# Three of the modulation vectors weighed on VectorE, the latents' squares added before the matmul, and a token-wise final norm

## What is computed

```python
for l in range(2):
    sh1, sc1, g1, sh2, sc2, g2 = split(silu(c) @ w_mod[l] + b_mod[l], 6)   # latents
    mod_c = silu(c_ctx) @ w_mod[l] + b_mod[l]                              # context, all six only in layer 0
    xn = rmsnorm(h, norm1_g[l]) * (1 + sc1) + sh1                          # xnc likewise
    proj = xn @ w_in[l]               # pooling, Hyena, q and kv latents, gates
    q = rmsnorm(c_q, q_norm_g[l]) @ w_uq[l]; kv = rmsnorm(c_kv, kv_norm_g[l]) @ w_ukv[l]
    h = h + g1 * token_mix(...)       # three branches, gated, then w_out
    h = h + g2 * (relu((rmsnorm(h, norm2_g[l]) * (1 + sc2) + sh2) @ w_ff1[l]) ** 2 @ w_ff2[l])
return rmsnorm(h, final_g)
```

## Time and profile before

| | |
|---|---|
| median of 3 runs | 1388.97 us (1387.62 to 1389.35) |
| the profiled execution: its time, its span | 1388.05 us, 1386.2 us |
| PE, PE weight load, DVE, ACT, POOL busy (us) | 1352.0, 1109.7, 779.5, 549.4, 195.1 |
| chain that ended last, by engine | PE 92%, DVE 3%, ACT 2%, DMA 1%, issue 1% |
| mean granted clock of PE | 0.994 |

### The profile page before, as it was taken

One profiled execution on the slowest core, in us unless ns is written; L12 is line 12 of the kernel. 1 busy time (PEld: TensorE's weight loads), 2 busy tenths in 40 slices (PEclk: granted clock), 3 DMA queues, 4 the chain that ended last, 5 costly groups with the idle time before them and its releaser, 6 DMA issues.

```text
span 1386.2 us, 19645 instructions
## 1 busy us (share of the span) xinstructions
PE 1352.0 (98%) x8084; PEld 1109.7 (80%) x8084; DVE 779.5 (56%) x1127; ACT 549.4 (40%) x849; POOL 195.1 (14%) x179
## 2 busy tenths in 40 slices
PE   7999999999999999999999999999999999999997
PEld 3567766778778886877778888888779999899996
DVE  5555575234448666543223443477866788765663
ACT  5652472332233323432112432143555445553552
POOL 1251000703100142000000002300005404100012
PEclk9999999999999999999999999999999999999998
DMA  9333303444531372345443235324325647455551
GB/s 374 119 131 114 107 1 141 155 167 160 205 107 61 122 263 102 107 152 183 152 143 109 98 117 214 124 81 140 107 79 190 223 138 278 143 190 185 184 195 62
DMA packets 55289, 205.28 MB, mean 148 GB/s; under 512 B 6261, under 2 KB 6645, under 8 KB 53664
## 3 DMA queue, kind: packets, MB, share of 16 engines
q1 hardware_dynamic: 52992, 194.22, 40.4%
q0 software_dynamic: 2208, 9.81, 2.0%
HBM read 200.86 MB, written 3.15 MB: 147 GB/s over the span
## 4 chain that ended last, share of the span: by engine, by line
PE 92%; DVE 3%; ACT 2%; DMA 1%; issue 1%; POOL 0%; SPq 0%; DVEq 0%; ACTq 0%
PE ps L1556 27%; PE ps L1558 26%; PE ps L1557 26%; PE ps L1868 2%; PE ps L1585 2%; PE ps L1879 1%; DMA pairs<-in_pairs 1%; PE ps L1894 1%; PE ps L1966 1%; PE ps L1978 1%; DVE wl L1040 1%; PE ps L1810 1%; PE ps L1706 1%; PE ps L1610 1%; DVE rstd L1078 0%
## 5 line engine op out<-in xcount | busy, mean ns | idle before, releaser
L1040 DVE TENSOR_TENSOR wl<-raw,wh 128x1024 fp32r<-128x1024 f32 (+2 forms) x272 | 353.5, 1302 | 220.4 <-ACT wh L723 217.1
L1556 PE MATMUL ps<-xh,wh 128*128 128x512 f32 (+2 forms) x1392 | 474.3, 341 | 2.2 <-DVE xl L1107 1.4
L1557 PE MATMUL ps<-xl,wh 128*128 128x512 f32 (+2 forms) x1392 | 466.5, 335 | 0.0
L1558 PE MATMUL ps<-xh,wl 128*128 128x512 f32 (+2 forms) x1392 | 466.3, 335 | 0.0
L723 ACT ACTIVATE wh<-raw 128x1024 fp32r<-128x1024 f32 (+2 forms) x272 | 283.7, 1043 | 321.5 <-PE ps L1558 320.4
L1556 PEld LDWEIGHTS ps<-xh,wh 128*128 128x128 f32 (+1 forms) x1392 | 261.0, 188 | 44.7 <-issue 14.7
L1558 PEld LDWEIGHTS ps<-xh,wl 128*128 128x128 f32 (+1 forms) x1392 | 261.4, 188 | 29.2
L1557 PEld LDWEIGHTS ps<-xl,wh 128*128 128x128 f32 (+1 forms) x1392 | 262.0, 188 | 28.0 <-issue 1.2
L1556 PE MATMUL ps<-hid_h,wh 128*128 128x512 f32 (+1 forms) x512 | 172.5, 337 | 0.0
L1557 PE MATMUL ps<-hid_l,wh 128*128 128x512 f32 (+1 forms) x512 | 171.7, 335 | 0.0
L1558 PE MATMUL ps<-hid_h,wl 128*128 128x512 f32 (+1 forms) x512 | 171.6, 335 | 0.0
(11 more groups left out here) (252 smaller groups left out, 1441.7 us busy)
## 6 DMA issues: line engine op xcount, KB each, us to landing
raw<-in_units SPq DMA_DIRECT2D x262, 512.0 KB, 3.3
...
```

Of the source, the lines that this page charges most:

```text
L1040: dve.tensor_tensor(wl[:, g % SLOTS, 0:n], raw[:, g % SLOTS, 0:n], wh[:, g % SLOTS, 0:n].bitcast(F), ALU.subtract)\
L1556: pe.matmul(dst, w_h, m_h, start=first, stop=False)
L1557: pe.matmul(dst, w_h, m_l, start=False, stop=False)
L1558: return pe.matmul(dst, w_l, m_h, start=False, stop=last)
```

## The change

Three separate edits.

1. Of the ten modulation vectors, numbers 7, 8 and 9 (`SUMMED`: layer 1's first scale, first gate, second shift) are weighed on DVE. For each of a vector's eight units DVE multiplies the 128x1024 unit by the silu column and adds it into an accumulator (`weigh`); vector 7 is needed for both streams and takes two such operations a unit, 8 and 9 one: 32 in all. Then PE adds up the partitions with a 128x32 matrix that holds one column of ones (`mod_sum`, 8 matmuls for vector 7, 4 for the others). The patterns of layer 0 change: no modulation in `ff1a`, one weighing behind each of the 16 units of `ff2a` and the first 8 of `ff2b`, three sums (`s`), and a tail of 8 units (vector 10 on PE) where there were 13. A ring slot comes free when its unit is weighed, so SP waits on that.
2. DVE adds up the latents' squares (two additions for q, one for kv), and PE sums one block where it summed three and two, and 4 columns where it made 8.
3. The last norm is made token by token: PE turns the gained blocks (16 transposes), sums squares into one column a token block, ACT takes two roots of 128x1, DVE one reciprocal of 128x2, and DVE and ACT each scale half of the output from PSUM and store it, in four pieces from SP and ACT.

```diff
-            return pattern if first else pattern.replace("m", "").replace("t", "")
+            return pattern if first else pattern.replace("m", "").replace("t", "").replace("s", "")
...
-            ("ff1a", with_mods("MMMMMMMMmmMMMmmMMMmmMMmm")), ("ff2a", with_mods("MMmmMMMmmMMMmmMMMmmMMmmMMMm")),
-            ("ff1b", 16 * "M"), ("ff2b", 16 * "M" + with_mods(13 * "t")),
+            ("ff1a", with_mods("MMMMMMMMMMMMMMMM")), ("ff2a", with_mods("MmMmMmMmMmMmMmMmMmMmMmMmsMmMmMmMm")),
+            ("ff1b", 16 * "M"), ("ff2b", with_mods("MmMmMmMmsMmMmMmMmMMMMsMMMM" + 8 * "t")),
...
+            elif kind == "s":
+                p.after[j].append(("sum", mod // KB - 1))
+                p.after[j].append(("copy", mod // KB - 1))
+                order.append(("sum", mod // KB - 1))
+                turn, lead = mod // KB - 1, 0
+            elif mod // KB in SUMMED:
+                p.after[j].append(("weigh", mod))
+                order.append(("unit", mod))
+                mod += 1
...
-GAP_SLOTS = {i: (layer, name, slot) for layer, name, count in ((0, "w_out", 14), (0, "ff2b", 11), (1, "w_out", 6))
+GAP_SLOTS = {i: (layer, name, slot) for layer, name, count in ((0, "w_out", 14), (0, "ff2b", 8), (1, "w_out", 6))
...
-GAP_COUNTS = {(0, "w_out"): 14, (0, "ff2b"): 25, (1, "w_out"): 31}
+GAP_COUNTS = {(0, "w_out"): 14, (0, "ff2b"): 22, (1, "w_out"): 28}
...
+        weighted_of = {7: gained[:, :, :].rearrange("p a b -> p (a b)").rearrange("p (s c) -> p s c", c=D),
+                       8: final[:, 0:1, :], 9: final[:, 1:2, :]}
...
-                        sp.wait_ge(mod_done, RING[RING.index(i) - MOD_SLOTS] - MOD_FIRST + 1)
+                        before = RING[RING.index(i) - MOD_SLOTS]
+                        if before // KB in SUMMED:
+                            sp.wait_ge(weighed, weighed_before(before) + streams_of(before // KB))
+                        else:
+                            sp.wait_ge(mod_done, DONE["unit", before])
...
-            pieces = (slice(0, 4), slice(4, 6), slice(6, 8))
-            for piece in pieces:
-                for m in range(piece.start, piece.stop):
-                    await_normed(sp, 2 * DEPTH, m)
-                sp.dma_start(out[:, piece, :], gained[:, piece, :]).then_inc(out_stored, 16)
-            sp.wait_ge(out_stored, 16 * len(pieces))
+            for tb in range(SEQ // 128):
+                sp.wait_ge(final_dve, tb + 1)
+                sp.dma_start(out[tb, :, 0:512], final[:, tb, 0:512]).then_inc(out_stored, 16)
+            sp.wait_ge(out_stored, 16 * (SEQ // 64))
...
+                act.wait_ge(mod_done, DONE["sum", v] if v in SUMMED else DONE["unit", KB * v + KB - 1])
...
+                if v == 2 * DEPTH:
+                    for tb in range(SEQ // 128):
+                        act.activation(rstd[:, tb:tb + 1], ps[:, tb, 0:1], ACT.Sqrt, bias=eps[:, 0:1], scale=1.0 / D).then_inc(std_ready, 1)
+                    return
...
+            act.wait_ge(rstd_ready, parts_before(2 * DEPTH) + 1)
+            act.wait_ge(gain_turned, 1)
+            for tb in range(SEQ // 128):
+                act.activation(final[:, tb, 512:D], ps[:, FINAL_BANK[tb][1], :], ACT.Copy, scale=rstd[:, tb:tb + 1]).then_inc(final_act, 1)
+            for tb in range(SEQ // 128):
+                act.wait_ge(final_act, tb + 1)
+                act.dma_start(out[tb, :, 512:D], final[:, tb, 512:D]).then_inc(out_stored, 16)
...
+            def weigh(i):
+
+                v, k = divmod(i, KB)
+                before = weighed_before(i)
+                if k == 0:
+                    dve.wait_ge(mod_done, DONE["unit", KB * SUMMED[0] - 1])
+                weight, loaded, value = mod_slot(i)
+                dve.wait_ge(loaded, value)
+                for st in range(streams_of(v)):
+                    acc, by = weighted_of[v][:, st, :], silu_wide[:, k, st:st + 1]
+                    if k == 0:
+                        dve.tensor_scalar(acc, weight, by, None, ALU.mult).then_inc(weighed, 1)
+                    else:
+                        dve.wait_ge(weighed, before - streams_of(v) + st + 1)
+                        dve.scalar_tensor_tensor(acc, weight, by, acc, ALU.mult, ALU.add).then_inc(weighed, 1)
 
             def add_mod(v):
...
-                        dve.wait_ge(mod_done, GAP_XL_LAST - MOD_FIRST + 1)
+                        dve.wait_ge(mod_done, DONE["unit", GAP_XL_LAST])
...
-                v = 2 * DEPTH
-                norm_rstd(v)
-                for m in range(KB):
-                    if m not in BY_POOL:
-                        dve.wait_ge(gain_ready, m + 1)
-                        dve.tensor_tensor(gained[:, m, :], gained[:, m, :], rstd[:, 0:SEQ], ALU.mult).then_inc(normed_dve, 1)
+                count = parts_before(2 * DEPTH)
+                dve.wait_ge(std_ready, count + 2)
+                dve.reciprocal(rstd[:, 0:2], rstd[:, 0:2]).then_inc(rstd_ready, 1)
+                dve.wait_ge(rstd_ready, count + 1)
+                dve.wait_ge(gain_turned, 1)
+                for tb in range(SEQ // 128):
+                    dve.tensor_scalar(final[:, tb, 0:512], ps[:, FINAL_BANK[tb][0], :], rstd[:, tb:tb + 1], None, ALU.mult)\
+                       .then_inc(final_dve, 1)
...
+                def add_queries():
+                    chained(dve.tensor_tensor(lat_sq[:, 0, 0:n], lat_sq[:, 0, 0:n], lat_sq[:, 1, 0:n], ALU.add))
+                    dve.tensor_tensor(lat_sq[:, 0, 0:n], lat_sq[:, 0, 0:n], lat_sq[:, 2, 0:n], ALU.add).then_inc(lat_added, 1)
+
+                def add_keys():
+                    dve.wait_ge(lat_sq_ready[layer], QB + KVB)
+                    dve.tensor_tensor(lat_sq[:, QB, :], lat_sq[:, QB, :], lat_sq[:, QB + 1, :], ALU.add).then_inc(lat_added, 1)
...
                             split(WAVE + i + 1)
+                    add_queries()
+                    add_keys()
...
                             i += 1
+                    add_queries()
+                    add_keys()
...
+            def mod_sum(v):
+
+                vectors_ready(pe, v - 1)
+                if v == SUMMED[0]:
+                    pe.wait_ge(picks_ready, 2)
+                pe.wait_ge(weighed, weighed_before(KB * v) + KB * streams_of(v))
+                for st in range(streams_of(v)):
+                    for j in range(4):
+                        mm = pe.matmul(ps[32 * j:32 * j + 32, mod_bank(v), 0:MOD_COLS], picks[:, 1 - st:33 - st],
+                                       weighted_of[v][:, st, j * MOD_COLS:(j + 1) * MOD_COLS], start=st == 0, stop=st == streams_of(v) - 1)
+                mm.then_inc(mod_done, 1)
...
+            def turn_gained(m):
+                pe.wait_ge(gain_ready, m + 1)
+                for tb in range(SEQ // 128):
+                    mm = pe.transpose(ps[:, FINAL_BANK[tb][m // 4], m % 4 * 128:m % 4 * 128 + 128], gained[:, m, tb * 128:(tb + 1) * 128], ident)
+                return mm
+
+            def final_sums(v):
+
+                def by_token(squares, first, last):
+                    for tb in range(SEQ // 128):
+                        mm = pe.matmul(ps[:, tb, 0:1], squares[:, tb * 128:(tb + 1) * 128], ones[:, 0:1], start=first, stop=last)
+                    return mm
+
+                for m in range(KB - 2):
+                    turn_gained(m)
+                pe.wait_ge(act_bank_free, drained(DEPTH - 1, "ff1b"))
+                pe.wait_ge(squares_added, added_before(v + 1))
+                by_token(sq_sum, True, False)
+                pe.wait_ge(h_squared, squared_before(v + 1))
+                by_token(sq[:, 0, :], False, False)
+                turn_gained(KB - 2)
+                pe.wait_ge(last_squared, v)
+                by_token(sq[:, 1, :], False, True).then_inc(sumsq_ready, 1)
+                turn_gained(KB - 1).then_inc(gain_turned, 1)
...
-                for first, count, bank, nt in ((0, QB, 4, n), (QB, KVB, 5, T)):
-                    pe.wait_ge(lat_sq_ready[layer], first + count)
-                    for k in range(count):
-                        mm = pe.matmul(ps[:, bank, 0:nt], ones, lat_sq[:, first + k, 0:nt], start=k == 0, stop=k == count - 1)
-                    mm.then_inc(lat_sumsq[layer], 1)
+                for i, bank, nt in ((0, 4, n), (QB, 5, T)):
+                    pe.wait_ge(lat_added, 2 * layer + (2 if i else 1))
+                    pe.matmul(ps[:, bank, 0:nt], ones, lat_sq[:, i, 0:nt], start=True, stop=True).then_inc(lat_sumsq[layer], 1)
                 for tb in range(T // 128):
-                    for k in range(KVB):
-                        mm = pe.matmul(ps[:, 7, tb:tb + 1], lat_sq[:, QB + k, tb * 128:(tb + 1) * 128], ones[:, 0:1],
-                                       start=k == 0, stop=k == KVB - 1)
+                    mm = pe.matmul(ps[:, 7, tb:tb + 1], lat_sq[:, QB, tb * 128:(tb + 1) * 128], ones[:, 0:1], start=True, stop=True)
                 mm.then_inc(lat_sumsq[layer], 1)
...
-                rms(2 * layer + 2)
                 if layer == 0:
```

(3 more changed lines are left out.)

49 lines of the change are left out of this document (30 added, 19 removed).

## The result

The changed kernel takes 1376.64 us (median of 4 runs, 1376.35 to 1377.87), the kernel before 1389.16 beside it. The ratio is 0.9915, with a 95% interval of 0.9901 to 0.9929: 11.8 us faster by the ratio. 1369.2 was forecast, so 7.4 us are missing, and the time lies outside the range.

The account below looks back on a forecast made before the run. PE, busy 98% of the span, was taken as the bound. 9.4 + 1.0 + 6.0 + 1.6 + 2.0 = 20.0 us off the profiled 1388.05 gave 1368.0, or 1369.2 for the median; range 1366.5 to 1375.

Parts of the forecast that it names:

- a unit of 24 is 5.44 us: Layer 0's `ff2a`: PE starts a weight matmul every 0.227 us, so 24 take 5.44 us, with no wait.
- not free, or the units cost nothing: Rival, 0.03: the weighing isn't free or the units cost nothing where they stood; PE waits elsewhere, so no change.
- The inline units and the tail: Modulation units leaving `ff1a` and `ff2a` gain 9.4 us; eight tail units instead of 13 between the layers gain 1.0.
- The weighing: DVE's 32 operations of 128x1024 take 1.3 us each; DVE keeps up, cost on the path 0.
- Latents, layer 0: At layer 0's latents' sums three wide and four narrow matmuls leave PE: 3.4 us gained, nothing waits.
- 0.75 each at most: Layer 0: DVE's two q additions, 0.75 us each at most, fall into its 1.47 us wait for ACT.
- Layer 1: At layer 1's latents' sums PE sheds matmuls worth 2.6 us; a late DVE could eat up to 1 us.
- the rival with VectorE as the bound: Rival, 0.12: DVE's additions and reciprocals become layer 1's bound; the tail's 1.0 and 1.0 of the sums go: 1371.2.
- The clock: Behind layer 1's sums PE's clock no longer falls, because the change halves the thin stretch ahead: 1.6 us gained.
- The rival's fall in a new place: Rival, 0.25: the clock falls anyway or newly, with PE waiting in layer 1's first wave: 1370.8 or 1372.4.
- The end: The last norm, token by token: first store at 1379.15 instead of 1381.20, gain 2.0 us.
- The low bound: The last norm's gain is only 0.5 us, because ACT's first DMA of the kernel is slow.

Follow-up runs that it names:

- e1: The changed kernel with the new buffer `picks` allocated behind all others, so every other buffer stands where it stood before the change: 0.9872 of the kernel before.
- e2: The kernel before with only an unused buffer of 144 bytes a partition behind `wl`, which moves the buffers behind it as the change does: 1.0069.
- e8: e1 with 28 of the weighings cut to 8 of 1024 columns: 0.9861 of the kernel before.
- e3: The kernel before with only the addition of the latents' squares on DVE, no buffer moved: 0.9956.
- e13: e1 with layer 0's keys' addition placed behind `ckl` on VectorE: 0.9855 of the kernel before.
- e9: e1 with the four one-column matmuls at the latents' sums issued twice each: 0.9875 of the kernel before.
- e15: e1 with the wide float32 sums issued five times and the one-column matmuls twice, as before the change: 0.9902 of the kernel before.
- e5: The kernel before with an unused buffer of 64 bytes a partition behind `wl`: 1.0014.
- e7: The kernel before with only the token-wise last norm: 0.9982.
- e6: e1 without the token-wise last norm: 0.9885 of the kernel before.
- e12: e1 measured once more, the same program: 0.9864 of the kernel before.

## Why the prediction was wrong

**The step that failed** is in the part on the bound: "a unit of 24 is 5.44 us", with 0.227 us a step, was carried over into the changed kernel as a constant, and what the diff does to the other buffers' addresses was put at nothing. The step depends on where the operands lie, and the diff moves them (e1, e2). By the table, after against e1 loses 2.5 us up to 540 us (`cq`, `ck`, `fh`), 2.8 in `ff2a` and 2.8 in `ff2b`. In layer 1 the 767 steps on `hid` cost 0.0022 more each, 1.7 us, which shorter steps on `xh` more than covered this time. By the ratios it is 0.0043 to 0.0051, 6 to 7 us of the 7.4. None of my rivals had it: "not free, or the units cost nothing" looked for a wait, and there is none.

**The inline units and the tail:** 9.4 + 1.0 forecast. In e1 the saving goes from 4.3 at 540 us to 14.1 ahead of layer 1's sums: 9.8. It is made of 11.4 up to `ff2b`, 2.5 lost on its two sums and turns, 1.4 won in the tail and 0.6 lost between layer 1's first weight matmul and its sums. The sum of vector 7 stands 1.33 us apart from its neighbours (700.68 to 702.01) where a pair stood 1.32. **The weighing:** 1.3 taken, 1.28 measured, cost on the path 0, shown by e8. One of 28 took over the 2 us that the prediction named as a sign of being wrong (2.31, beside GpSimd); e8, which shortens it too, shows that it cost nothing. **The tail:** PE waits for `xl` as described, but starts 0.26 us behind its end at 911.35, where 0.1 was forecast.

**Latents, layer 0:** 3.4 forecast, 2.5 measured (e3 and the table). The step that fell is "0.75 each at most" for the additions "into the 1.47 us": beside GpSimd's rows they took 1.67 to 1.79, against 0.68 for the same shape in layer 1 with GpSimd idle, and I had not seen that the sums' own bank waits for `ckl`. The earlier trace rows had shown the price, 1.99 for 1.32. The Trainium skill ("SBUF — State Buffer", "SBUF: two separate sides") says that a VectorE operation with two SBUF inputs and a GpSimd operation that reads SBUF exclude each other for a whole instruction. The rows agree: the second and third addition and GpSimd's operations end by turns, each addition 0.55 us behind GpSimd's (79.14 and 79.69, 80.86 and 81.40), and `ckh` and `ckl`, which read PSUM, keep their 0.74 and 0.75 beside GpSimd. That the sums waited for `ckl` is shown by e13: with the keys' addition behind it the whole 3.5 us (6.23 - 2.76) are there. That GpSimd made `ckl` late is read from the rows; no run takes GpSimd's operations away. **Layer 1:** 2.6 forecast, 2.6 measured. The additions ended at 937.1, 0.7 us ahead of the sums, so the rival with VectorE as the bound did not come.

**The clock:** the 1.6 us came (from 8.2 to 9.8 in the table). The cause I named is not borne out: in e9 the thin matmuls are back, in e15 the whole stretch is, and the clock stayed, in one profile each. Of the four profiles with the old tail and the old stretch three show the fall (before, e2, e5) and one does not (e7); none of the others does, e3 with the old tail and the short stretch among them. What brings it, and whether it belongs to the old kernel or to an execution, stays open; so the 1.6 us are not certain in each run. Other executions of before hint at the execution: of the 23 beside e5 to e8, 12 took 1384.0 to 1385.9 us at a mean granted clock of 0.995 to 0.997, and 11 took 1387.0 to 1389.2 at 0.993 to 0.994. The mean does not say where in the kernel the clock was low. The rival's fall in a new place did not come: in the wave five of PE's steps stretch to 0.19 to 0.22 us behind the first `xl`, and the granted clock stays at 1.00.

**The end:** 2.0 forecast; 2.7 in the spans (18.9 - 16.2), 2.5 by e7, 1.8 by e6. The first store is issued 4.4 us behind the last weight matmul (4.5 forecast). The low bound had a slow first DMA of ScalarE, which no run shows: its two stores landed 2.8 and 3.4 us behind their issue, SyncE's two 2.9 and 3.5. **Not in the forecast:** the first weight matmul came 1.6 us earlier, which is no gain of the change, since e2 with the code of before has 27.60 there and e12 with that of e1 has 29.20. It goes with the granted clock in the first microseconds, from 25 to 27 us in before, e12 and after:

```profile
25.00:27.00 2.00, 2.00 (x4) 0.94 (x3) 1.96 (x2) 1.33 (x2) 0.00 (x0) 0.50 1.00 412
25.00:27.00 2.00, 2.00 (x3) 0.67 (x2) 2.00 (x3) 1.18 (x2) 0.00 (x0) 0.50 0.99 403
25.00:27.00 2.00, 2.00 (x7) 0.98 (x6) 2.00 (x3) 1.01 (x2) 0.00 (x0) 1.00 0.99 406
```

And e1 gives back 2.1 us between `cqh` of layer 1 and the end, in steps of 0.1178 on `xh`. This is mostly e1's chance: the stretch took 412.7 us in before, 414.8 in e1, and 411.8 to 413.1 in e6, e8, e12 and e13. For e1, 9.8 + 2.5 + 2.6 + 1.6 + 2.7 + 1.9 (the start) - 2.1 is 19.0, the 18.9 of the two spans.
